# Dilated attention: where three reciprocals, three bank waits and the outcome weights' split stand in their queues

## What is computed

```
def block(q_blk):                                   # first attention
    s = einsum('bqhgd,bkhd->bhgqk', q_blk, k_all)
    p = softmax(s, axis=-1)
    return einsum('bhgqk,bkhd->bqhgd', p, v_all)
y_lat = o @ w_o

qkv = (xn @ w_qkv).reshape(B, S, 3, G, Hg, dh)      # dilated attention, G = 3, Hg = 8, dh = 64
for g, (window, dilation) in enumerate(((128, 1), (512, 4), (2048, 16))):
    s = einsum(q_blk, k_blk) * dh ** -0.5 ; s = where(mask, s + bias, NEG)
    lse = logsumexp(s) ; p = exp(s - lse) ; o = einsum(p, v_blk)
wts = softmax(stack(lses), axis=0)                  # over the three groups
o = einsum('gbshd,gbsh->bshd', outs, wts) @ w_o
```

## Time and profile before

| | us |
|---|---|
| median of three runs | 2317.73 |
| lowest and highest run | 2315.89, 2319.3 |
| profiled execution | 2308.6 |
| its span, first to last instruction | 2307.2 |
| PE busy in it | 2145.3 (93%) |
| DVE, ACT busy | 1294.5 (56%), 1033.8 (45%) |
| mean granted PE clock | 0.971 of full speed |

### The profile page before, as it was taken

The page is one execution under the profiler, slowest core; times in us unless marked ns, Lnnn a source line. Parts: engine busy times, 40 slices in busy tenths (PEclk is TensorE's granted clock), DMA queues, the critical chain, the costliest instruction groups (busy, mean ns, idle before and its releaser), DMA issues.

```text
span 2307.2 us, 31359 instructions
## 1 busy us (share of the span) xinstructions
PE 2145.3 (93%) x13248; PEld 1646.3 (71%) x13248; DVE 1294.5 (56%) x1837; ACT 1033.8 (45%) x1501; POOL 134.7 (6%) x112
## 2 busy tenths in 40 slices
PE   6879989999996998999889999998999998999997
PEld 4656754577774765777667888886777776888885
DVE  2467755666637775355536766435255446766633
ACT  3446632155525664377744433324233355433321
POOL 0012200000001220000010000003000002000000
PEclk9879999999997999999999999999999999999998
DMA  9889980022217995211012222222222112312210
GB/s 400 328 336 374 381 338 0 1 110 95 91 37 280 353 357 220 109 38 37 37 73 110 104 79 110 105 97 66 75 94 92 49 42 94 121 74 110 110 55 37
DMA packets 40574, 324.17 MB, mean 141 GB/s; under 512 B 7231, under 2 KB 8255, under 8 KB 21695
## 3 DMA queue, kind: packets, MB, share of 16 engines
q1 hardware_dynamic: 27288, 288.91, 32.6%
q0 software_dynamic: 10624, 25.71, 3.2%
q10 hardware_dynamic: 2512, 7.41, 0.8%
HBM read 310.40 MB, written 24.19 MB: 145 GB/s over the span
## 4 chain that ended last, share of the span: by engine, by line
PE 85%; DVE 6%; ACT 4%; DMA 2%; issue 2%; POOL 0%; SPq 0%; ACTq 0%; DVEq 0%; POOLq 0%
PE PS L163 80%; PE PS L911 2%; PE PS L661 1%; DVE work L2360 1%; ACT work L1606 1%; PE PS L1172 1%; DMA tokens<-work 1%; DVE WR L2366 1%; ACT work L1611 0%; ACT L1611 0%; DMA work<-ys 0%; DMA work<-in_xtok 0%; ACT work L1602 0%; DMA work<-tokens,slots 0%; DVE work L2421 0%
## 5 line engine op out<-in xcount | busy, mean ns | idle before, releaser
L163 PE MATMUL PS<-HS,RS 128*128 128x512 f32 x4128 | 953.0, 392 | 11.2 <-DVE HS L2137 8.6
L163 PEld LDWEIGHTS PS<-HS,RS 128*128 128x128 f32 x4128 | 775.1, 189 | 177.7 <-issue 13.7
L1780 DVE TENSOR_TENSOR RS<-ring,RS 128x1024 fp32r<-128x1024 f32 x212 | 258.9, 1224 | 345.0 <-ACT RS L1268 345.0
L1268 ACT ACTIVATE RS<-ring 128x1024 fp32r<-128x1024 f32 x212 | 221.6, 1052 | 255.7 <-PE PS L163 255.7
L1703 ACT ACTIVATE work<-work,vec 128x512 f32<-128x512 f32 x88 | 71.9, 818 | 239.6 <-DVE work L2484 239.6
L1780 DVE TENSOR_TENSOR CR<-ring,WR 128x1024 fp32r<-128x1024 f32 x128 | 153.2, 1221 | 36.0 <-ACT WR L1268 33.5
L163 PE MATMUL PS<-work 128*64 128x128 f32 (+5 forms) x1728 | 131.8, 294 | 28.5 <-DVE work L1839 19.9
L1268 ACT ACTIVATE WR<-ring 128x1024 fp32r<-128x1024 f32 x128 | 134.8, 1058 | 51.5 <-PE PS L163 45.8
L1268 ACT ACTIVATE work<-PS 128x384 f32<-128x384 f32 (+2 forms) x194 | 86.8, 485 | 125.1 <-PE PS L1172 41.9
L163 PEld LDWEIGHTS PS<-work 128*64 128x64 f32 (+2 forms) x1728 | 107.5, 147 | 48.0 <-issue 31.6
L163 PE MATMUL PS<-RS,HS 128*128 128x512 f32 x480 | 114.7, 397 | 8.2 <-DVE HS L2137 8.2
(11 more groups left out here) (258 smaller groups left out, 2796.4 us busy)
## 6 DMA issues: line engine op xcount, KB each, us to landing
ring<-in_wexp SPq DMA_DIRECT2D x32, 2048.0 KB, 10.8
ring<-in_wmod SPq DMA_DIRECT2D x24, 2048.0 KB, 10.1
ring<-in_ffnu SPq DMA_DIRECT2D x22, 2048.0 KB, 8.2
ring<-in_wexp SPq DMA_DIRECT2D x32, 1024.0 KB, 11.1
ring<-in_ffnd SPq DMA_DIRECT2D x10, 2048.0 KB, 7.2
ring<-in_dilqk SPq DMA_DIRECT2D x6, 2048.0 KB, 8.1
ring<-in_sbqk SPq DMA_DIRECT2D x4, 2048.0 KB, 8.4
ring<-in_dilv SPq DMA_DIRECT2D x3, 2048.0 KB, 8.0
```

The source lines that it names most:

```text
L163: return T.matmul(out, l, r, start=start, stop=stop, skip_group_check=True)
L1268: return S.activation(out, x, ACT.Copy, **kw)
L1780: V.tensor_tensor(lo, src, hi.bitcast(F32), ALU.subtract).then_inc(w_lo, 1)
```

## The change

Three moves, no instruction more or less.

1. In the first attention DVE's split of the first three `wo` units leaves step 30. Two units are split behind `ada(23)`, ahead of `outcome(7)`; the third goes with the loop behind it. ACT's part stays in step 30.
2. PE's one wait for all four copies of the last values' banks, ahead of `project_qk(0)`, becomes three: the first unit (bank 4) waits for one copy, the second (bank 5) for two, the third (bank 7) for all four.
3. In the dilated attention's steps 3, 7, 11 and 15 `rcp_sums(u)` stands ahead of `most(u + 1)` instead of behind it (in step 15 there is no `most` and nothing moves).

```
@@ dilated, on PE
-            pe.wait_ge(pr_c, 20)
...
                     if i < 3:
+                        pe.wait_ge(pr_c, 16 + (1, 2, 4)[i])
                         pe.wait_ge(sm_ta, 64 + rot + i - 2)
@@ attention, on DVE
                 if u == 30:
                     affine(1, 1)
-                    split_lo("wo", ahead("wo", 0, False))
             ada(23, TURN[128 % 3])
+            split_lo("wo", part_of["wo"].start + 2)
             outcome(7, a_o, a_rl, 0)
             finish(7)
@@ dilated, on DVE
                 if (u + 1) % 4 == 0 and u + 1 < 16:
                     project_qk((u + 1) // 4)
+                if u % 4 == 3:
+                    rcp_sums(u, st, rl, 8)
                 if u + 1 < 16:
                     most(u + 1, 0)
                     most(u + 1, 1)
-                rcp_sums(u, st, rl, 8)
+                if u % 4 < 3:
+                    rcp_sums(u, st, rl, 8)
```

## The result

| | before | after |
|---|---|---|
| median of four runs, us | 2317.27 | 2294.72 |
| lowest and highest run | 2315.89, 2319.3 | 2292.13, 2297.54 |
| profiled execution | 2308.6 | 2297.54 |
| its span | 2307.2 | 2296.1 |
| its mean granted PE clock | 0.971 | 0.969 |

The ratio of the times is 0.9902 (0.9885 to 0.9919): the changed kernel is 22.7 us faster, with an interval of 18.8 to 26.6. 2303.3 was predicted, with 2299 as the lowest; the direction was right and the gain 8 us larger than the sum of 14.4. The two profiled executions differ by 11.1 us only. For after it was the slowest of its four runs, and for before it was faster than all of its four. So the trace has to say two things: what the edits did at their places, and why the timed runs gained more.

What follows compares the result with a forecast made beforehand. PE, busy 93% of the span, was taken as the bound, with 13.4 us of idle at three places. 4.2 + 3.7 + 6.5 = 14.4 us off the 2317.7 median gave 2303.3 us, range 2299 to 2310.

Steps and rivals of the forecast that it cites:

- the sum of 14.4: All three places together: 4.2 + 3.7 + 6.5 = 14.4 us saved, 11.4 if the two clock falls were absent.
- the last one: Whole kernel: the 14.4 us from the profiled execution (2308.6) taken off the timed median (2317.7), giving 2303.3 us.
- The lower end of the range, 2299: Whole kernel: forecast less the timed runs' 3.4 us spread and the 1.2 us of the reciprocals' upper end.
- Part 3: Dilated attention, reciprocals ahead of the next maximum: 2.17 us at each of three places, 6.5 us.
- The bounds of 3.3 and 7.7: Dilated attention reciprocals: 3 x 2.57 = 7.7 us above; 3 x 1.09 = 3.3 below, if only spreading slips into the idle.
- Part 1: First attention's last turn: 3.15 us of idle and 1.08 us of clock, 4.2 us; lower end 3.1.
- the cover of `outcome(7)`: First `wo` product: 2.7 us of cover against at most 0.4 us delay from two splits ahead on DVE.
- Part 2: Banks ahead of first q and k: 1.8 us of wait and 1.9 of clock, 3.7 us; lower end 1.8.
- The doubt: At 1696.4, 2.9 us idle left the clock at 1.00; both falls might be absent from timed runs, sum 11.4 us.
- The rival in which the steps go to half clock: Dilated steps of the changed kernel: half clock costs 1.08 us a step, 17.3 over 16, losing the gain; chance 0.02.
- The other rivals: Clock not back, 2306.3 (0.16); reciprocals' gain given back, 2306.5 (0.08); last turn's wait moved, 2307.5 (0.06); banks without effect, 2307.0 (0.03).
- the one at 1696.4: Dilated step 0: a 2.9 us PE idle behind which the clock might fall instead, within the 2306.3 us rival, chance 0.16.

Runs made afterwards that it cites:

- the one with the falls: The kernel before profiled again, nothing edited: 2316.51 us, ratio 1.0005; its dilated steps took 194.54 us.
- the fill: Kernel before plus useless PE products, 12 in the wait ahead of the first attention's last turn and 9 in the wait for the banks: 2314.28 us, ratio 0.9996.
- kernels with fills: Useless PE products in waits: before with the last-turn and bank waits filled, 2311.45 and 2314.28 us; changed kernel with nine other waits filled, longer version, 2294.55 us.
- the second's 19.5: The changed kernel once more, nothing edited, against before: 2295.66 us, ratio 0.9916, 19.5 us faster (16.2 to 22.5).

## Why the prediction fell short

**The step that failed is the last one**, from the profiled execution to the median. Before's timed runs stood 9.1 us above its profiled execution "for a reason the page doesn't show", and the prediction took "the same 14.4 us off the median". The reason lay at the places of the change: in most executions the clock falls behind the three waits on the reciprocals, and in the profiled one it did not. Six executions with those waits left idle were profiled, 18 places; 12 fell: all three in three executions, two, one and none in the others. Taking the waits away also took away those falls, 5.5 us where all three fall. The lower end of the range, 2299, rested on the 3.4 us that three timed runs spread; over all its runs before spreads from 2304.6 to 2323.3.

**Part 3** is therefore the term that was mis-sized: 6.5 us predicted, 6.51 measured against the first execution, 12.0 against the one with the falls. The bounds of 3.3 and 7.7 came from the rows of one execution and could not hold that. The place was read rightly: spreading without a wait, then 0.39 us on L2423, three times.

**Part 1**: 4.2 predicted, 4.28 measured. The turn without an idle, the 1.74 us and the cover of `outcome(7)` came as stated. Of the 4.28 the clock is 1.1, as the fill shows. It was there in four of six executions; in the two without a fall the same stretch is 27.4 us long, and the part is worth 3.2.

**Part 2**: 3.7 predicted, 3.32 measured. The idle left is 0.82 us (some 0.7 was stated), and the first unit takes 5.83 instead of 5.4. The clock's share is 1.6, not 1.9 (7.43 - 5.37 - 0.1 is 1.96, which was written as 1.9).

**The doubt was pointed the wrong way.** The row with an idle of 2.9 us at a clock of 1.00 was read as "the two falls of this profile needn't have been in the timed runs", which lowers the gain. The same row says that an idle of 2.57 us without a fall, in one execution, may fall in others, which raises it. The Trainium skill ("TensorE: Matmul & The Clock Gate", Part 1: The HAM clock gate) says that the watch over PE runs free of the kernel; the trace agrees with that: one program showed no fall at the three places in one execution and three in the next. The rival in which the steps go to half clock was right on the mechanism and had it in the wrong kernel.

**The other rivals** did not come: in the changed kernel the clock came back at both of its places, ACT's rounding held nobody, and the first unit did not wait for its weights. The fall at another idle, the one at 1696.4, came only in kernels with fills.

**What stays open.** The places explain 19.8 us against an execution with all three falls. The first comparison's 22.7 and the second's 19.5 both agree with that within their intervals. But not every execution has all three: on the mean of the six executions that kept each wait the stretches are 28.3, 39.5 and 192.8 us, and the places explain 17.7, which lies in the second interval and 1.1 us below the first. The rest of the first comparison is not accounted for. The trace of after and that of before differ also in stretches that nothing touched, in both directions (the rows of L2146 behind the first expert stage take 19.1 us instead of 21.1 from first start to last, those behind the second 31.7 instead of 29.1), and which of these differ on average was not settled.

## What to carry to other kernels

A wait of PE costs its length and the slow clock behind it, here 1.1 to 2.7 us a fall for waits of 2.6 to 3.2 us, and one profiled execution need not show the second part: where the profiled execution is faster than the timed runs, compare the granted clock at the places of the change in a second one before carrying a sum from one to the other. A wait that can't be moved can be filled with useless products a little shorter than the wait; in the executions shown this kept the clock at the place, though in two the fall then came at a later idle, and a fill that is too long can give the gain back.

## What the runs showed of the hardware

An idle of 2.57 us at one and the same instruction brought PE to 1.2 GHz in 12 of 18 cases (the clock fell in the idle or up to 1.6 us after work had begun again); behind the idle of 2.56 us ahead of the first q and k the clock fell in each of the six executions that kept it, and behind the 3.15 us in the attention in four of six (the two with fills at the reciprocals' waits took 27.42 and 27.43 us for part 1's stretch, against 28.5 to 29.0 in the others). The idle of 2.99 us in step 0 saw it in three of 13. So in these counts a longer idle is not the surer fall. Where the idle of part 1, of the banks or of the reciprocals had been filled, shortened to 0.82 us or less, or taken away, no execution shows a fall behind that place. A product of two 128x128 f32 tiles is recorded as two matmuls, together 0.24 us (16 products, 32 records, 3.83 us). And with only 0.82 us of idle ahead of it, the first q unit of the changed kernel still takes 5.83 us where the next takes 5.37; where that 0.5 us goes was not looked into.
